# A mixture of experts whose experts' room is counted in units of 32 rows, with strips of 64 and 32 columns in one block, and first loads in another order

## What is computed

```
def hier_moe(t, w_group, b_group, w_expert, b_expert, w1, w3, w2):
    g_idx = argmax(softmax(t @ w_group + b_group))         # one of 4 groups
    top_v, top_i = top_k(expert logits of that group, 2)   # two of its 8 experts
    gates = softmax(top_v) * g_p
    # every expert e of 32, over the tokens that chose it:
    #   h = silu(xb @ w1[e]) * (xb @ w3[e]);  y = h @ w2[e]
    # w1, w3: 1024 x 512, w2: 512 x 1024, all float32
    # out[token] += gate * y
```

## Time and profile before

| | us |
|---|---|
| median of 3 runs | 5239.36 |
| lowest and highest | 5226.63, 5248.02 |
| profiled execution | 5218.35 |
| its span | 5216.6 |

### The profile page before, as it was taken

One profiled execution on the slowest core, in us unless ns is written; L12 is line 12 of the kernel. 1 busy time (PEld: TensorE's weight loads), 2 busy tenths in 40 slices (PEclk: granted clock), 3 DMA queues, 4 the chain that ended last, 5 costly groups with the idle time before them and its releaser, 6 DMA issues. The chain is left out here.

```text
span 5216.6 us, 91144 instructions
## 1 busy us (share of the span) xinstructions
PE 4360.9 (84%) x37874; PEld 2559.6 (49%) x37874; DVE 2263.2 (43%) x3060; ACT 1221.1 (23%) x2005; POOL 452.7 (9%) x407
## 2 busy tenths in 40 slices
PE   5688868978889795999956988699688879599993
PEld 0344434657777453444423444366577765344441
DVE  0265525756656553111132655377455556311113
ACT  0122115752222110010101221177222222001011
POOL 0033320000000000000010333100000000000001
PEclk7899977989999896999978999799899989699997
DMA  9567552013222334899965575400322223489995
GB/s 388 178 162 206 154 195 69 22 50 109 60 60 61 137 125 176 331 378 394 406 241 197 160 212 153 121 27 18 118 59 59 77 61 142 185 331 378 410 405 210
DMA packets 253650, 941.94 MB, mean 181 GB/s; under 512 B 38604, under 2 KB 101580, under 8 KB 226664
## 3 DMA queue, kind: packets, MB, share of 16 engines
q1 hardware_dynamic: 195032, 757.72, 39.5%
q0 software_dynamic: 23616, 93.86, 6.4%
q10 hardware_dynamic: 34640, 84.96, 4.2%
HBM read 727.72 MB, written 169.44 MB: 172 GB/s over the span
## 5 line engine op out<-in xcount | busy, mean ns | idle before, releaser
L755 PE MATMUL ps<-w,hT 128*128 128x480 f32 (+1 forms) x2240 | 910.5, 566 | 23.9 <-DMA hT<-s_hT 22.5
L2497 PE MATMUL ps<-w,xT 128*128 128x512 f32 (+1 forms) x2272 | 796.1, 597 | 7.5 <-DVE xT L2438 7.5
L755 PEld LDWEIGHTS ps<-w,hT 128*128 128x128 f32 x2240 | 436.3, 197 | 475.3 <-issue 425.1
L2497 PEld LDWEIGHTS ps<-w,xT 128*128 128x128 f32 (+1 forms) x2272 | 313.5, 169 | 443.0 <-issue 432.5
L2443 DVE TENSOR_TENSOR sg<-sg,ps 128x512 f32<-128x512 f32 x56 | 38.5, 687 | 1088.4 <-ACT sg L2239 1088.4
L2497 PE MATMUL ps<-w,hT 128*128 128x512 f32 (+1 forms) x1136 | 394.8, 594 | 3.3 <-ACT hT L2230 3.3
L1074 DVE TENSOR_REDUCE nm<-ps 128x1 f32<-128x1280 f32 (+1 forms) x216 | 295.8, 1369 | 174.5 <-PE ps L1165 174.4
L1165 PE MATMUL ps<-KT,qs 32*128 32x512 f32 (+3 forms) x1200 | 283.3, 589 | 95.6 <-DMA KT<-s_qkT 71.3
L1032 ACT ACTIVATE work<-ps,nm 128x1280 f32<-128x1280 f32 (+1 forms) x216 | 265.8, 1231 | 119.4 <-DVE nm L1074 115.2
L2009 PE MATMUL ps<-w_out,yT 128*128 128x512 f32 x576 | 255.0, 601 | 16.1 <-ACT yT L1857 16.1
L2497 PEld LDWEIGHTS ps<-w,hT 128*128 128x128 f32 (+1 forms) x1136 | 154.7, 168 | 203.8 <-issue 198.5
(11 more groups left out here) (292 smaller groups left out, 5477.9 us busy)
## 6 DMA issues: line engine op xcount, KB each, us to landing
w<-in_e_w SPq DMA_DIRECT2D x192, 2048.0 KB, 15.4
wt<-in_w_mod SPq DMA_DIRECT2D x16, 3072.0 KB, 25.5
s_ye<-yo ACTq DMA_DIRECT2D x56, 512.0 KB, 10.7
w<-in_w_in ACTq DMA_DIRECT2D x12, 1920.0 KB, 17.8
ra<-s_scan SPq DMA_DIRECT2D x160, 128.0 KB, 2.7
kb<-s_scan SPq DMA_DIRECT2D x160, 128.0 KB, 2.7
x<-s_x SPq DMA_DIRECT2D x36, 512.0 KB, 7.8
pf<-po SPq DMA_DIRECT2D x20, 840.0 KB, 5.3
```

Source lines behind the costliest of these rows:

```text
L755: mm = pe.matmul(ps[:, c, 0:n], hT[i % 2][:, t, :], w[:, c, t, 0:n], start=(t == 0), stop=(t == DT - 1))
L2497: mm = pe.matmul(ps[j * m:(j + 1) * m, bank, :], xs[:, t, j * m:(j + 1) * m], w[:, t, cols], start=(t == 0), stop=(t == nt - 1), skip_grou ...
```

## The change

It has two parts.

**The experts' room.** The room of each rank is now a number of units of 32 rows (`ROOM`), and `ORDER` is a list of groups of experts: a digit is an expert's room in units, and the experts of a group stand one after the other in whole blocks. "62" is an expert of 192 rows and one of 64 in two blocks, "31" one of 96 and one of 32 in one block, "93" one of 288 and one of 96 in three. The plans have 25 and 21 blocks. The parts of a block are cut into aligned strips of 128, 64 or 32 rows (`strips`), each a matmul of its own on as many columns of the array. Layer 0 has 14 blocks with one strip, 6 with 64/64 and 5 with three strips (four 64/32/32, one 32/32/64); layer 1 has 7, 6 and 8 (seven and one). A product still runs over the steps outside and the strips inside. DVE finds `base` and `cap` of each rank from a table (`k_room`) by comparing and reducing over 32 x 32.

**First loads.** Input projection: the w_in chunks and gains are loaded by SP behind x, gain, G and S of one condition and ident; G and S of the other condition follow after the first tile, as does their part of DVE's work; the chunks of the attention columns are loaded by SP too. Attention: the first queries go on ACT's queue; where a context part comes first, only its 256 keys are loaded before it, the rest behind the second tile's queries; the first queries of the next part are loaded ahead; the five constants go on POOL's queue, V behind the first keys; PE waits for V only at the first product with it. The zeros of `s_ye` are stored in the scan phase of layer 0, in 68 pieces of 256 KB. The diff, cut:

More of the change, by code:

```diff
@@ L44 @@
 SLOTS = TOK * 2
-ORDER = ["THDHDHSSSHSSSHSSSHSSSHSSS", "DHDHDHSSHSSSHSSHSSSHSSHS"]
-BLOCKS = [sum({"T": 3, "D": 2}.get(c, 1) for c in o) for o in ORDER]
-def most_over(layer):
-    slots, half = (TOK if layer < DEPTH - 1 else SEQ) * 2, 2 * ORDER[layer].count("H")
-    return half + (slots - half * (P // 2 + 1)) // P + 1
+UNIT = 32
[5 more added lines that the diff above has]
+BLOCKS = [sum(-(-sum(int(c, 16) for c in g) // 4) for g in o) for o in ORDER]
+def most_over(layer):
+    left, n = (TOK if layer < DEPTH - 1 else SEQ) * 2, 0
+    for cost in sorted(UNIT * u + 1 for u in ROOM[layer]):
+        if cost < P and cost <= left:
+            left, n = left - cost, n + 1
+    return n + left // P + 1
 TRIO = 3
@@ L1249, in tile @@
                                 place = 2 * pt.nc if g < GROUPS else pt.nc
+                                if first and g == 1 and pt.k0 == 0:
+                                    pe.wait_ge(v_in, 16)
                                 if g < GROUPS and pt.nc > 1:
@@ L2071, in expert_phase @@
     n = NT - t0
-    blocks, ranks, (nT, nD, nS) = expert_plan(layer)
+    blocks = expert_plan(layer)[0]
     K = len(blocks)
@@ L2130, in expert_phase, with done_in @@
         XB, UP, DN, TH = 0, 2, 4, 6
+        def done_in(k):
+            return sum(final for *_, final in blocks[k])
         def overflow(eng, block):
@@ L2204, in _ @@
                 pool.wait_ge(table_done, 1)
-                for k, (row0, _, _, _) in enumerate(blocks):
+                for k in range(K):
                     b = k % NX
@@ L2513, in put_out @@
                     for c in range(2):
-                        mm = product(DN + c, hT, ws, HF, slice(c * 512, (c + 1) * 512))
+                        mm = product(DN + c, hT, w2, strips(blocks[k]), HF, slice(c * 512, (c + 1) * 512))
                     mm.then_inc(down, 1)
@@ L2518, in _ @@
                 turn_x(xg[0])
-                for k, (_, pos, first, final) in enumerate(blocks):
+                for k in range(K):
                     pe.wait_ge(xT_done, k + 1)
@@ L2684, in constants @@
         "k_pos": np.array([expert_plan(layer)[1] for layer in range(DEPTH)], np.float32),
+        "k_room": np.array([[16 * u + c for u, c in zip(expert_plan(layer)[2], ROOM[layer])] for layer in range(DEPTH)],
+                           np.float32),
         "k_j_row": np.arange(OVER).astype(np.float32),
```

140 lines of the change are left out of this document (62 added, 78 removed).

## The result

The changed kernel takes 5345.73 us (median of 4 runs, 5340.48 to 5354.97) against 5234.24 for the kernel before (4 runs): ratio 1.0212, interval 1.0184 to 1.0240. It is slower by 111.5 us; whether by more than 2%, the interval leaves open. The forecast was slower, 5335. The profiled executions are 5348.93 us (span 5347.1) and 5218.35 (span 5216.6), 130.6 us apart.

The account below looks back on a forecast made before the run. PE was taken to set the time in both expert phases. Terms 147 + 25 + 7 - 28 - 40 - 12 = +99 us, on the median 5338, stated as 5335; 8 in 10 range 5235 to 5420.

Parts of the forecast that it names:

- Shape changes serialise: Expert phases, mixed 64/32/32 blocks: each tile-shape change drains the array, 0.15 us; a step 2.02 us; together +147 us.
- Rival A: Mixed expert blocks: strips of 64 and 32 columns run side by side, a block costs 23 us; 4985 us; chance 0.15.
- Rival C: Mixed expert blocks: 32-wide strips don't pair, a step is 0.86 us longer; 5600 us; chance 0.02.
- Two-expert blocks in a row: Layer 1's experts, three such blocks in a row twice: PE waits 12.5 us for weights, twice, +25 us.
- Routing: Room by table: more DVE operations on the chain to the first gather, +3.5 us a layer, +7.
- First products: Input projections' first loads, moved from ACT to SP: PE starts earlier, -14 us a layer, -28 in all.
- the cover that was taken for free: Input projection: PE's first products hide constants queued behind w; if that fails, up to 5 us, not counted.
- the attention columns' loads: Input projection's last tile: these loads move from ACT to SP and wait for the same products, 0 us.
- Attention, layer 0: First loads there: first scores earlier, -16 us, and four later waits go, -24; -40 in all.
- Layer 1: Its attention's first loads: whole keys still load first, only query issues and V are out of their way, -12 us.
- Zeros in the scan: Layer 0's scan: 68 stores of 256 KB by POOL hide behind PE, 0 us, though they could cost up to 15.
- Rival D: Experts: one load above its room, three overflow blocks run, some 60 us each; 5515 us; chance 0.03.

Follow-up runs that it names:

- the four-strip kernel: The changed kernel with every strip 32 columns wide in blocks with a part of 32 or 96 rows; 5046.04 us, ratio to before 0.9654.
- The run that forced it by accident: The four-strip kernel, loading only the first quarter of w2 from the fourth expert on, so outputs differ; 5134.98 us (one run).
- run 64: Not a run's label: in "Four 32-wide strips run 64 MATMULs" the word is a verb, and 64 counts the MATMULs, which take 7.00 us.

## Why the prediction was right

- **Shape changes serialise** (0.76): right, with the size. A step was put at 2.02 us and is 1.985; 0.134 us a change instead of 0.15. A mixed block costs 49.4 us (50.3): 21.96 + 3 x (15.88 - 6.87) + 0.45. Five and eight of them with the others give 692 and 686 us, and PE was busy 693 and 696; some 5 of layer 1's 10 us are the slow clock behind the waits (below). The Trainium skill's rule that changing the tiling mode drains the engine (TensorEngine Tiling (Array Packing), Key Properties) held in this trace, 64 to 32 columns included; its next rule there, that tiles operate independently, held among tiles of one shape (7.00 us for four strips).
- **Rival A** (strips side by side) fell on the disjoint columns. For strips that run side by side it forecast 4985; the four-strip kernel, where they do, took 5046. Against its own kernel before that is a gain of 180 us and not of 254. Of the missing 74, 48 lie in the expert phases, where PE waits 62 us for weights; the rest lies outside them.
- **Rival C** (32-wide strips don't pair) fell by the same rows: the two 32-wide strips of a step take 0.98 us together, the 64-wide one 1.00. The 0.17 us a MATMUL of the earlier trace rows, which I took for a rate in an expectation, was read at a granted clock of 0.67; at 1.00 it is 0.11 (7.00 / 64).
- **Two-expert blocks in a row**: 25 forecast, 33.2 measured, at the blocks named (14.2 and 14.3 instead of 12.5 each, then 3.7 and 1.1 for blocks I had not named). Behind each of the first three waits TensorE ran for a while at the lower of its two clock levels (granted clock 0.92 on the mean from 4706 to 4723, 0.78 from 4865.5 to 4874), which cost some 5 us more: 17.35 and 17.52 instead of 15.95 us, 8.96 instead of 7.09. Three blocks in a row turned out not to be the condition, though: with two in a row a "31" behind a "22" waited 10 and 12 us.
- **Routing**: +7 forecast; with the mix before it the two stretches grew 4.5 and 4.3.
- **First products**: -28 forecast, -34 measured. So 6 more came in than forecast. Behind the first products two terms were too good: the cover that was taken for free failed twice (4.1 and 5.9), and the attention columns' loads cost 4 a layer instead of 0 (15.5 and 14.8 us of waits where 11.2 and 11.3 were). Both steps failed for one reason: I had read what a queue must issue, and not what stands ahead of an item that comes late in it.
- **Attention, layer 0**: -40 forecast, -34.6 measured. The waits fell by 39.9 (from 40.8 and 18.9 to 19.8), so the term was right; PE was busy 366.39 us for matmuls that had taken 361.12, which took 5 back. **Layer 1**: -12 forecast, and the wait fell by 4.3 only. All keys are loaded as before, and the DMA engines run full in the wait (a share of 1.00 from 3344 to 3364; 0.85 from 3341 to 3365 before). Ident, now issued behind the queries on ACT's queue, lands last: 17.0 us from issue to landing, 1.7 before. PE's timeline:

```profile
3364.43 4.93 PE L1176 MATMUL ps<-KT,qs 64*128 64x512 f32 x12 [26.20 <-DMA ident<-in_k_ident]
```

  This step of the prediction failed: "out of their way" was wrong, for the bytes are the same on whichever queue they go. Whether ident issued ahead of the queries would have saved more was not tried. Then the phase itself was 5.5 us longer, with PE busy 318.84 us instead of 313.33 for the same matmuls.
- **Zeros in the scan**: 0 forecast, the scan 7.9 us longer. That the zeros did it was not shown. Windows of both layers' scans before:

```profile
1189.00:1766.00 577.00, 488.93 (x11907) 429.77 (x11904) 339.88 (x441) 154.51 (x229) 4.84 (x9) 0.95 0.25 74
3719.00:4308.00 589.00, 502.91 (x11906) 441.85 (x11902) 339.53 (x440) 154.32 (x229) 3.27 (x6) 0.93 0.24 72
```

  Layer 0's after, with the zeros in it:

```profile
1142.00:1727.00 585.00, 495.88 (x11907) 435.82 (x11904) 340.39 (x441) 154.48 (x229) 40.99 (x77) 0.94 0.33 104
```

  Layer 1's in the kernel that finishes one size first:

```profile
3686.00:4264.00 578.00, 487.70 (x11906) 428.41 (x11902) 339.70 (x440) 154.18 (x229) 3.27 (x6) 0.95 0.25 72
```

  Some 11906 matmuls, the same in all four, keep PE busy 488 to 503 us, as the granted clock goes from 0.95 down to 0.93. Layer 1's scan, the same in all kernels, took from 578 to 596 us in their profiles; layer 0's took 576 and 582 without the zeros and 576 to 590 with them. If they cost anything, it is less than this spread.
- **The sum.** On the profiled executions +99 was forecast and +130.6 measured, on the medians +111.5. The median came out near because I had added 21 us for the kernel before's median over its profiled execution; after the change the profiled one (5348.93) lies 3 above its median. The forecast 5335 is thus closer than its working, by luck: the terms were short by 12 on the medians and by 31 on the profiled executions. The expert phases have no part in that: 172 us forecast for both, 172.2 measured, 6 under in layer 0 and 6 over in layer 1, where 8 us of waits and 5 of slow clock more than forecast stand against mixed blocks that were each 0.9 us cheaper. That the two cancel is luck as well. The 31 us are the differences of the other stretches from their terms, each under 10.
- **Rival D** (overflow) did not come. The run that forced it by accident priced its group at 144 us for three blocks, 48 each; the rival had 60.

## What to carry to other kernels

Parts of unequal width in one TensorE block were free here only when the strips had one width: cut all of them to the smallest (here 32 columns, four side by side, 7.00 us, where 128 takes 6.87) instead of to the largest that fits. Ask of every plan that saves blocks whether the loop over strips changes the shape, and count the changes: 0.13 us each, and the overlap that is lost in between. Once PE is relieved, look for the next bound: here 223 MB a layer of weights and rows, over buffers that come free in pairs.

## What the hardware showed beyond the forecast

- The price of a change is nearly the same between 64 and 32 columns as between 128 and 64 (0.13 against 0.15 us), and linear in their number (15, 8 and 1 in a product).
- Two sizes exclude each other on disjoint columns of the array too: 1.985 us a step for a 64-wide strip and two 32-wide ones beside it.
- Four 32-wide strips run 64 MATMULs of 512 columns in 7.00 us, 0.11 us each, at a granted clock of 1.00.
- The same matmuls of one scan differ by 3% in busy time from kernel to kernel through stretches at a granted clock of 0.50. Terms under some 10 us of this kernel can't be read from one profile's stretch lengths, only from their waits.
